# Local attention: values as the stationary operand, transposed probabilities streamed, scaling moved to ScalarE

## The reference, cut to what matters

```python
s = einsum('bnqgrd,bnkgd->bngrqk', qb, kw) * scale       # masked band, plus cached keys
p = softmax(concatenate([s_loc, s_ctx, s_sink], axis=-1))
out = einsum('bngrqk,bnkgd->bnqgrd', p[..., :L], vw) + einsum('bngrqk,bkgd->bnqgrd', p[..., L:L+Lc], cv)
```

## Time and profile before

| what | value |
|---|---|
| median of three runs | 4006.52 us |
| the profiled execution's own time | 3995.5 us |
| its span | 3993.7 us |
| PE busy | 3697.8 us (93%) |
| DVE busy | 2609.3 us (65%) |
| ACT busy | 680.5 us (17%) |
| POOL busy | 1616.5 us (40%) |

### The profile page before, as it was taken

How to read it: one execution, slowest core, us unless ns; L and a number is a source line. 1 busy time by engine, 2 the same in 40 slices (tenths; PEclk the granted TensorE clock), 3 DMA queues, 4 the chain that set the end, 5 groups by cost and what they waited for, 6 DMA issues and landing times. The chain is left out here.

```text
span 3993.7 us, 40043 instructions
## 1 busy us (share of the span) xinstructions
PE 3697.8 (93%) x13766; PEld 2139.0 (54%) x13766; DVE 2609.3 (65%) x5973; ACT 680.5 (17%) x1534; POOL 1616.5 (40%) x1498
## 2 busy tenths in 40 slices
PE   2988978999999999999979888889999999999997
PEld 1556676655555555554445666766555555555543
DVE  5786588776666666677724738978677646566444
ACT  1031356500000000000012224652000000000000
POOL 0030055445566544444402002553677655444330
PEclk7987999999999999999989799999999999999998
DMA  6321134579999999999930131447899999989783
GB/s 222 122 95 50 74 96 138 158 291 406 374 380 374 377 372 378 376 377 355 372 129 2 44 117 38 133 138 254 340 410 410 390 364 344 367 338 359 290 308 130
DMA packets 364809, 1026.96 MB, mean 257 GB/s; under 512 B 30784, under 2 KB 132416, under 8 KB 363840
## 3 DMA queue, kind: packets, MB, share of 16 engines
q0 software_dynamic: 147456, 536.94, 35.1%
q1 hardware_dynamic: 117424, 433.99, 28.5%
q10 hardware_dynamic: 99728, 53.48, 4.8%
HBM read 965.07 MB, written 59.22 MB: 256 GB/s over the span
## 5 line engine op out<-in xcount | busy, mean ns | idle before, releaser
L1835 PE MATMUL ps<-colsT,arena 128*128 128x384 f32 x4096 | 1358.7, 486 | 4.2 <-DMA arena<-in_peer_ut 4.2
L1835 PEld LDWEIGHTS ps<-colsT,arena 128*128 128x128 f32 x4096 | 775.9, 190 | 582.6 <-issue 94.7
L1870 PE MATMUL ps<-arena 128*128 128x512 f32 x1536 | 676.4, 592 | 0.0
L1349 POOL DMA_INDIRECT proj<-in_peer_u,eidx x336 | 460.0, 1369 | 244.0 <-DVE modbc L1541 116.1
L1349 POOL DMA_INDIRECT proj<-in_peer_v,eidx x335 | 359.5, 1073 | 315.7 <-DVE colsT L1552 216.9
L1870 PEld LDWEIGHTS ps<-arena 128*128 128x128 f32 x1536 | 291.8, 190 | 345.2 <-issue 317.6
L1335 POOL TENSOR_SCALAR x<-iota,modbc 128x128 f32<-128x128 f32 x192 | 145.0, 770 | 759.9 <-ACT modbc L1672 593.0
L1541 DVE CUSTOM_DVE_ANT_0 proj<-proj,rows 128x1024 f32<-128x1024 f32 x336 | 400.4, 1224 | 56.3 <-DMA proj<-in_peer_u,eidx 54.6
L1552 DVE SCALAR_TENSOR_TENSOR colsT<-proj,modbc,colsT 128x1024 f32<-128x1024 f32 x330 | 409.6, 1285 | 14.9 <-DMA proj<-in_peer_v,eidx 14.7
L1870 PE MATMUL ps<-arena,rows 128*128 128x512 f32 x768 | 337.8, 592 | 0.0
L1870 PE MATMUL ps<-arena,x 128*128 128x512 f32 x768 | 337.8, 592 | 0.0
(11 more groups left out here) (295 smaller groups left out, 3775.2 us busy)
## 6 DMA issues: line engine op xcount, KB each, us to landing
arena<-in_peer_ut SPq DMA_DIRECT2D x256, 512.0 KB, 6.7
arena<-in_peer_v SPq DMA_DIRECT2D x256, 512.0 KB, 6.7
gmat_d<-arena ACTq DMA_DIRECT2D x24, 2048.0 KB, 9.3
arena<-gmat_d SPq DMA_DIRECT2D x64, 768.0 KB, 8.7
proj<-in_w_adaT SPq DMA_DIRECT2D x48, 512.0 KB, 9.2
modbc<-in_w_adaT SPq DMA_DIRECT2D x30, 512.0 KB, 3.7
rows<-in_w_adaT SPq DMA_DIRECT2D x18, 512.0 KB, 3.5
arena<-in_w_in SPq DMA_DIRECT2D x2, 4224.0 KB, 17.4
```

The costliest lines, as they stand in the source:

```text
L1349: pool.indirect_dma_start(ring[slots[at]], None, tab, bass.IndirectOffsetOnAxis(ap=eidx[:, b * SLOTS + q:b * SLOTS + q + 1], axis=0)).then ...
L1835: mm = pe.matmul(ps[:, 2 + j % 2, 0:ND], utab[:, j % UR, k], hT[:, k, NG:T], start=(k == 0), stop=(k == KT - 1))
L1870: mm = pe.matmul(ps[:, Y_BANKS[2 * d + c2], :], wT[j % CR][:, d * P:(d + 1) * P], vtab[:, j % VR, c2 * 512:(c2 + 1) * 512], start=(j == 0) ...
```

## The change

`values` is turned round: the values are the weights (64 columns of the array, half `g` on PSUM partitions 64g to 64g + 63) and `probT` is streamed (128 columns). The output comes as features x queries for both halves of a pair, and `turn_y`, `yrow` and the semaphores `y_made` and `yt_done` go. Since a denominator now belongs to a column, the probabilities are scaled before they are transposed: DVE's `denominators(p)` makes the reciprocals in step p + 1, ahead of `head_max(p + 1)`, and ACT's `scaled(p)` multiplies both halves of `prob` in place in step p + 1, ahead of `exps(p + 1)`. `turn_probs(p)` waits for `pn_ready` of `scaled` in place of `p_ready` of `exps`; `copy_y(p)` waits for `values(p)`.

```diff
@@ PE
-                        pe.wait_ge(p_ready, i + 1)
+                        pe.wait_ge(pn_ready, i + 1)
...
-                            mm = pe.matmul(ps[:, 4 + p % 2, g * HD:(g + 1) * HD], probT[i % 4][:, n], vv[:, g * HD:(g + 1) * HD],
+                            mm = pe.matmul(ps[g * HD:(g + 1) * HD, 4 + p % 2, 0:P], vv[:, g * HD:(g + 1) * HD], probT[i % 4][:, n],
                                            start=(n == 0), stop=(n == len(keys[b]) - 1))
...
-                def turn_y(p):
-                    pe.wait_ge(y_made, p + 1)
-                    pe.transpose(ps[:, 4 + p % 2, P:2 * P], yrow[:, p % 2], ident[:, :]).then_inc(yt_done, 1)
...
-                    if s >= 3:
-                        turn_y(s - 3)
@@ ACT
+                def scaled(p):
+                    j, b = pairs_[p]
+                    act.wait_ge(rd_ready, p + 1)
+                    for g in range(2):
+                        i = 2 * p + g
+                        rows_ = prob[i % NP_][:, 0:len(keys[b])].rearrange("p n q -> p (n q)")
+                        act.activation(rows_, rows_, ACT.Copy, scale=den[:, i:i + 1]).then_inc(pn_ready, 1)
...
-                    act.wait_ge(yt_done, p + 1)
+                    act.wait_ge(av_done, p + 1)
...
-                    act.activation(dst, ps[:, 4 + p % 2, P:2 * P], ACT.Copy).then_inc(yt_sb, 1)
+                    act.activation(dst, ps[:, 4 + p % 2, 0:P], ACT.Copy).then_inc(yt_sb, 1)
...
                 for s in range(PSTEPS):
+                    if 1 <= s <= NPAIR:
+                        scaled(s - 1)
                     if s < NPAIR:
                         exps(s)
@@ DVE
-                def norm(p):
+                def denominators(p):
                     i = slice(2 * p, 2 * p + 2)
                     dve.wait_ge(p_ready, 2 * p + 2)
                     dve.wait_ge(es_ready, p + 1)
                     c.link(dve.tensor_tensor(den[:, i], den[:, i], es[:, i], ALU.add))
-                    c.link(dve.reciprocal(den[:, i], den[:, i]))
-                    dve.wait_ge(av_done, p + 1)
-                    if p >= 2:
-                        dve.wait_ge(yt_done, p - 1)
-                    dve.tensor_tensor(yrow[:, p % 2].rearrange("p (h e) -> p h e", h=2),
-                                      ps[:, 4 + p % 2, 0:P].rearrange("p (h e) -> p h e", h=2),
-                                      den[:, i].unsqueeze(2).to_broadcast([P, 2, HD]), ALU.mult).then_inc(y_made, 1)
+                    dve.reciprocal(den[:, i], den[:, i]).then_inc(rd_ready, 1)
...
+                    if 1 <= s <= NPAIR:
+                        denominators(s - 1)
                     if s < NPAIR:
                         head_max(s)
...
-                    if 2 <= s <= NPAIR + 1:
-                        norm(s - 2)
```

More of the change, by code:

```diff
@@ L189, in build @@
         sem("y_moved"), sem("x_landed"), sem("s_done"), sem("n_ready"), sem("p_ready"), sem("pt_done"), sem("pt_sb"))
-    av_done, y_made, yt_done, yt_sb, es_ready, gs_half, gs_done = (
-        sem("av_done"), sem("y_made"), sem("yt_done"), sem("yt_sb"), sem("es_ready"), sem("gs_half"), sem("gs_done"))
+    av_done, rd_ready, pn_ready, yt_sb, es_ready, gs_half, gs_done = (
+        sem("av_done"), sem("rd_ready"), sem("pn_ready"), sem("yt_sb"), sem("es_ready"), sem("gs_half"), sem("gs_done"))
     go_done, P_ready, gla_ready, gm_ready, gy_ready, sg_ready, pool_d = (
@@ L403, in build @@
         mx, ngm, den, es = (region(x, 256 + 40 * i, 40) for i in range(4))
-        yrow = region(x, 416, 2, P)
         kcb, modt = region(x, 1184, P), region(x, 1312, P)
```

## The result

The changed kernel takes 3976.31 us (median of 4 runs, 3975.09 to 3977.25), the kernel before 4006.89 us (4003.35 to 4010.41): ratio 0.9924, 95% interval 0.9906 to 0.9941. That is 30.6 us faster, where the forecast was 2.6 us slower and the range ended at 4000. The profiled executions have spans of 3973.7 and 3993.7 us, 20.0 apart: the profiled execution of the kernel before (3995.5 us) was 11 us faster than its median, that of the changed kernel (3975.85) was at its median.

What follows compares the result with a forecast made beforehand. In the two local-attention stages PE, DVE or waits between them bound different steps. Terms summed to 0.0 in layer 0 and +2.6 us in layer 1, added to the median 4006.5: 4009.1 us, 8-in-10 range 4000 to 4018.

Steps and rivals of the forecast that it cites:

- stretch 4: Steps 15 to 22: PE's wait ends last, and at the end DVE and PE in turn; no size given.
- term d: Steps 12 to 14, both layers: two norms leave DVE, one `denominators` comes, PE's transposes start later; -0.4 us each.
- Term g: PE's layout switches: 0 in filler steps, a loss where chunk work or gt follows; +1.0 us each layer.
- halves side by side: Rival: half 1 of `values` runs beside half 0, saving 14 us in PE-bound steps, 3995 us; chance 4%.
- a: Layer 0, steps 3 to 5: two norms leave the DVE chain, two `denominators` come; -1.8 us.
- signs of being wrong: `turn_probs` waiting over 0.5 us for ACT in filler steps, 12.4 us off a stage, or `values` at twice or half its time.
- b: Layer 0, steps 7 to 9: two norms go, one `denominators` comes, -0.8 us; layer 1: PE is last, 0.
- c: Steps 11 and 12, both layers: a norm goes from between the copies and `keys_out`; -0.6 us each.
- e: Step 18, both layers: `denominators` ahead of `head_max` on DVE delays the output gate's root; +0.39 us each.
- f: The tail, both layers: transposes of the last pairs wait for the scaling, less work at the end; +2.2 us each.
- one new ring: Rival: ACT's scaling precedes the transposes in every step; uncovered in steps 10 to 20, 29 us, 4036 us; chance 7%.
- All waits counted: Rival: DVE's chain sets the time everywhere, so 20.8 us of norm's waits and work go, 3986 us; chance 6%.

Runs made afterwards that it cites:

- e0: The kernel before, unchanged, run once more for a profile of another execution, which took 4001.0 us.
- e3: The kernel before with `values` streaming both heads' 128 columns, half of the output unread, all else as before: 3982.8 us, ratio 0.9946.
- e14: The kernel before with `values` streaming both heads' 128 columns only from pair 12 on (steps 14 to 19): 3986.6 us, ratio 0.9954.
- e4: The changed kernel with the two heads' `values` matmuls in turn, block by block, and one wait for both copies in front: 3982.8 us, ratio 0.9948.
- e1: The changed kernel with old `values`, a plain copy to `yrow` and `turn_y` put back, keeping ScalarE's scaling and the early sums: 4000.5 us, ratio 0.9984.
- e12: The changed kernel with the gate's 1/(1+e) made on ScalarE in place of VectorE's add and reciprocal: 3960.2 us, ratio 0.9882.
- e9: The kernel before with 9 extra matmuls, unused by the result, in step 13 of each layer: 4007.9 us, ratio 1.0005.
- e11: The changed kernel with VectorE's gate product cut into five pieces, one in each of steps 13 to 17: 3976.4 us, ratio 0.9928.
- e2: The kernel before with `values` swapped as in the change and no `turn_y`, the division by the sums left out: 3981.7 us, ratio 0.9939.
- e7: The changed kernel's scaling and early sums, but `values` in the old orientation streaming 128 columns, with row copy and `turn_y`: 3977.4 us, ratio 0.9936.
- e13: The kernel before with the gate's 1/(1+e) made on ScalarE in place of VectorE's add and reciprocal: 3973.6 us, ratio 0.9923.

## Why the prediction was wrong

**The step that failed** is the sum's silence on steps 15 to 17: no term stands there, so their change was put at 0. The prediction had them as PE's own (stretch 4), had `values` at 0.109 a record before and after ("weight-bound", then "stream-bound"), and so had nothing to add. It took the clock as a property of the place: term d has the work behind the reciprocal "at half the clock" on both sides. I had the row with 0.82 and 0.85 and said that PE runs at 1.2 GHz part of the time, but used it only as a factor on my terms. The change altered what PE streams in that stretch, and the time there is set by when full clock returns: 8.4 and 8.5 us in steps 15 to 17, -16.9 in all, where the sum has 0. In the second profile of before (e0) these steps took 36.0 and 28.4 us, so the two kernels differ there by 12 to 17 us. e3 shows that streamed columns alone do it; e14 that most of it is had by the streams of this stretch alone. Rows that could have warned me: PE 99% busy through step 15 and still at 0.50 (13.91 of 14.00 us).

**The price of `values`.** 0.109 a record was right for records in a row (head 1's last: (2161.86 - 2161.53)/3 = 0.11). "Side by side needs neighbours on different halves" was right as to order (e4: 1.02) and wrong at the seam, where the last records of one half and the first of the other overlap for nothing: 1.51, not 1.74 + 0.10. Term g (+1.0 a layer) did not appear; a 4-block pair beside a filler took 0.44 us less of PE. The rival "halves side by side" was therefore half true as to order. Its price, 14 us, was not to be had: with the halves fully side by side (e4) the kernel was 6.5 us slower than with the overlap at the seam alone.

**a** came out -0.3, not -1.8. The order was right (step 5 lost 1.4 us), but step 4 grew by 1.3 us (21.75 to 23.07), with ACT's scaled copies and its table load now in a row in front of `exps(4)`; I had only let the wait there "shrink little or nothing". PE's waits moved from the scores (4.05 and 4.18 us) to the transposes (5.45 and 1.86 us for ACT), in steps where a filler was to cover the scaling; that is one of the prediction's own signs of being wrong. **b** came out -2.0 and, in layer 1, where I had 0, -0.9 (PE is busy nearly throughout there). **c** was -2.6 and -3.4 for -0.6: norms and waits of DVE as I counted, but also a half-clock stretch that PE no longer falls into in layer 1 (step 12 granted 0.69 before, 1.00 after). **d** was -0.4 each, as forecast, and **e** +0.27 (0.4 forecast). **f** had the right sign and the right releaser (8.11 and 1.09 us for ACT), and was 0.7 to 1.0 instead of 2.2: against the copies of pair 17 the transposes of pair 18 came 1.4 us later (1.5 forecast), those of pair 19 2.0 (2.8 forecast). **Behind the stage** I had 0; it was +2.5 and +2.6; two executions of before differ by as much behind layer 0's stage, and layer 1's +2.6 stays open. The stages were to be 241.1 and 225.2 us long and were 228.5 and 210.2.

**The rival "one new ring"** (+29 us) is refuted as a net cost: e1 carries all of it, together with the early sums, and is 6 us faster than before. "All waits counted" (-20.8 us, 3986) came nearest in its number, but not by its reason: e1 holds that part, -6. (Of the 12.4 us of waits in it, have 11.3 for `values`.) The chances, added up, are 0.70 for the same time and 0.19 for slower, not 0.71 and 0.18.

**The median.** I added the change to the median of before, which hid 11 us: the changed kernel's runs agree within 2.2 us, before's lie in two groups. Why the changed kernel has one group wasn't tested.

**What stays open.** The runs show that wider streams in this stretch bring full clock back sooner; what in the chip counts them, they don't show. Nor do they show where the 10.6 us lie that separate the medians beyond the profiled 20.0.

## What to carry to other kernels

Where the granted clock of a stretch is 0.5 though PE is busy in it, don't price a change there by instruction durations alone: ask what it does to the streams, since the clock's return may be worth more than the work (here 17 us of 20 between the two profiles, and 19 to 24 us in the medians of e14 and e3). Fewer microseconds of matmul can cost time in such a stretch (e4), and wider streams that do nothing can win it (e3). Filling or moving a long wait paid here only where the clock held behind it (e12, not e9 and e11): look at the whole chain of the engine that is waited for, and try to give it to an engine that idles. And profile one kernel twice before reading microseconds off a single pair of profiles.

## What the runs showed of the hardware

- 16 records with 64-row outputs on the two column halves took 1.02 us in turn and 1.51 in two blocks, at full clock; in the old orientation 1.74.
- PE at 99% busy for 14.0 us at 1.2 GHz did not get full clock back with 64-column streams of `values` among the work (before, step 15, both layers); in another execution of the same kernel (e0, layer 1) it came back in that step, 12.3 us long. With 128-column streams it came back within that step in each of ten stages (changed, e2, e3, e7, e14).
- A fall needs no long wait right in front of it: in e13, layer 0, PE was busy 8.75 of 8.84 us in step 15, and step 16 (11.06 of 11.15 us busy) was at 1.2 GHz throughout.
- A wait of 0.97 us was followed by a fall of the clock in e4 and not in the changed kernel, which had the same wait one step later.
- 128x1280 on ScalarE (e12): a logarithm and an exponential of 1.27 us each, each behind a table load of 1.28, where VectorE's reciprocal takes 8.15.
